# A relative position bias moved from VectorE into the score matmuls, loaded by shifted reads, with some modulation chunks reordered

## The reference, cut to what matters

```python
bias = na_bias(na_rpb[l], in_win, dr_idx, dc_idx)     # [heads, 256 queries, 256 keys], from a 15 x 31 table per head
ya = merge_heads(na_latent(qa, ka, va, ka_c, va_c, bias, row_idx))
```

## Time and profile before

| what | before |
|---|---|
| median of 3 runs | 1964.91 us (1964.04 to 1965.57) |
| the profiled execution: time, span | 1964.91 us, 1963.0 us |
| TensorE busy | 1861.0 us (95%) |
| GpSimd busy | 1359.7 us (69%) |
| ScalarE busy | 935.7 us (48%) |
| VectorE busy | 737.9 us (38%) |
| share of TensorE in the chain that ended last | 85% |
| mean granted TensorE clock | 0.985 |

### The profile page before, as it was taken

One profiled execution on the slowest core, in us unless ns is written; L12 is line 12 of the kernel. 1 busy time (PEld: TensorE's weight loads), 2 busy tenths in 40 slices (PEclk: granted clock), 3 DMA queues, 4 the chain that ended last, 5 costly groups with the idle time before them and its releaser, 6 DMA issues.

```text
span 1963.0 us, 28180 instructions
## 1 busy us (share of the span) xinstructions
PE 1861.0 (95%) x9518; PEld 1483.9 (76%) x9518; DVE 737.9 (38%) x1323; ACT 935.7 (48%) x1464; POOL 1359.7 (69%) x780
## 2 busy tenths in 40 slices
PE   7987999989899999999999999999999899999997
PEld 5665788776688888677888886778888776778886
DVE  2276443257421125345111446452113646451112
ACT  4454544353454455565444545644445445644442
POOL 5504999650488878656988795478886884469883
PEclk9999999999999999999999999999999999999999
DMA  7747666567776655434766453346664453246661
GB/s 251 247 172 254 196 194 202 171 198 252 241 229 192 192 171 161 145 117 135 220 201 190 155 178 97 97 140 192 205 190 151 151 161 106 88 140 191 184 189 67
DMA packets 245560, 344.24 MB, mean 175 GB/s; under 512 B 20704, under 2 KB 140384, under 8 KB 245472
## 3 DMA queue, kind: packets, MB, share of 16 engines
q1 hardware_dynamic: 243328, 337.06, 54.1%
q10 hardware_dynamic: 2144, 6.03, 1.0%
HBM read 341.96 MB, written 1.05 MB: 175 GB/s over the span
## 4 chain that ended last, share of the span: by engine, by line
PE 85%; DVE 7%; ACT 3%; DMA 1%; issue 1%; POOL 1%; SPq 0%; ACTq 0%; DVEq 0%
PE bank L1990 24%; PE bank L1992 23%; PE bank L1991 23%; PE bank L2061 2%; PE bank L2536 2%; PE bank L2526 2%; PE bank L2553 2%; PE bank L2040 1%; ACT wh L671 1%; DVE xh L1185 1%; PE bank L2072 1%; PE bank L2229 1%; DVE xl L1187 1%; PE bank L2309 1%; DMA raw<-in_l_w_in 1%
## 5 line engine op out<-in xcount | busy, mean ns | idle before, releaser
L647 POOL TENSOR_TENSOR wl<-raw,wh 128x1024 fp32r<-128x1024 f32 x300 | 732.1, 2454 | 87.7 <-ACT wh L809 76.9
L1990 PE MATMUL bank<-wh,xh 128*128 128x512 f32 (+2 forms) x1746 | 692.7, 397 | 21.6 <-POOL wl L633 8.7
L1992 PE MATMUL bank<-wl,xh 128*128 128x512 f32 (+2 forms) x1746 | 674.1, 386 | 0.0
L1991 PE MATMUL bank<-wh,xl 128*128 128x512 f32 (+2 forms) x1746 | 673.8, 386 | 0.0
L632 POOL TENSOR_TENSOR wl<-raw,wh 128x512 fp32r<-128x512 f32 (+2 forms) x238 | 325.3, 1367 | 489.3 <-ACT wh L671 450.3
L809 ACT ACTIVATE wh<-raw 128x1024 fp32r<-128x1024 f32 x270 | 286.4, 1061 | 439.0 <-PE bank L1992 429.3
L1990 PEld LDWEIGHTS bank<-wh,xh 128*128 128x128 f32 x1746 | 329.7, 189 | 98.8 <-issue 27.7
L1992 PEld LDWEIGHTS bank<-wl,xh 128*128 128x128 f32 x1746 | 329.6, 189 | 68.0
L1991 PEld LDWEIGHTS bank<-wh,xl 128*128 128x128 f32 x1746 | 330.2, 189 | 62.0 <-issue 1.4
L671 ACT ACTIVATE wh<-raw 128x1024 fp32r<-128x1024 f32 (+2 forms) x268 | 274.2, 1047 | 206.9 <-PE bank L1992 134.5
L633 POOL TENSOR_TENSOR wl<-raw,wh 128x512 fp32r<-128x512 f32 (+2 forms) x238 | 318.2, 1337 | 0.0
(11 more groups left out here) (316 smaller groups left out, 1677.1 us busy)
## 6 DMA issues: line engine op xcount, KB each, us to landing
raw<-in_w_ffn_in SPq DMA_DIRECT2D x264, 256.0 KB, 2.9
raw<-in_w_in SPq DMA_DIRECT2D x224, 256.0 KB, 2.9
raw<-in_w_mod SPq DMA_DIRECT2D x192, 256.0 KB, 3.9
raw<-in_w_ffn_out SPq DMA_DIRECT2D x132, 256.0 KB, 2.9
raw<-in_l_w_gate SPq DMA_DIRECT2D x88, 256.0 KB, 3.7
raw<-in_l_w_up SPq DMA_DIRECT2D x88, 256.0 KB, 4.3
raw<-in_l_w_down SPq DMA_DIRECT2D x88, 256.0 KB, 2.9
raw<-in_l_w_in SPq DMA_DIRECT2D x48, 256.0 KB, 4.4
```

What stands on the lines that cost most here:

```text
L647: nc.gpsimd.tensor_tensor(wl[:, s, :], raw[:, s, :], words(wh)[:, s, :], ALU.subtract)\
L1990: mm(dst, x_hi, w_hi, start=first, stop=False, skip_group_check=True)
L1991: mm(dst, x_lo, w_hi, start=False, stop=False, skip_group_check=True)
L1992: return mm(dst, x_hi, w_lo, start=False, stop=last, skip_group_check=True)
```

## The change

1. The host passes the raw table (`rpb`, 2 x 8 x 15 x 31 floats) instead of the expanded one. `load_bias` reads it with overlapping rows: for each head two DMAs, each to 64 partitions, of 6 x 64 floats per partition. Partition p begins one float later than partition p-1, so queries come out in reversed order within each half of 64. That makes 16 DMAs for a layer in runs of 256 bytes, instead of 4 in runs of 3072 bytes.
2. A constant `flip` (two 64 x 64 exchange matrices) turns the order back. In every near step of the x streams two matmuls (128 x 128 by 128 x 256, float32) with `flip` write the bias into the two banks, and the score matmuls on the x keys add to that (`start` false). The additions and their waits on VectorE go. TensorE waits for `bias_set` ahead of the first score.
3. Modulation chunks of layer 1: 4 instead of 6 ahead of `mix1`, 2 in every `mla` step (two more in all), none within `out1` (four fewer), 8 instead of 4 in `mod1_norm`. One chunk of `uq` is computed ahead of the turn of the second latent, and ScalarE's limits for its copies follow.

```diff
+    put("flip", np.kron(np.eye(2), np.eye(64)[::-1]))
+    w, u = 63 - np.arange(P)[:, None] % 64, np.arange(64)[None, :]
...
-    plan.modulation("mod1_in", 1, w_mod[1], 6)
+    plan.modulation("mod1_in", 1, w_mod[1], 4)
...
-        plan.modulation(f"mod1_mla{u}", 1, w_mod[1], 1 if u in (2, 8) else 2)
-    plan.gemm("out1", a["l1_w_out"], [512] * 2, pair=0, k_groups=[range(2, KD), range(0, 2)], modulated={0: each[0]})
-    plan.modulation("mod1_norm", 1, w_mod[1], 4)
+        plan.modulation(f"mod1_mla{u}", 1, w_mod[1], 2)
+    plan.gemm("out1", a["l1_w_out"], [512] * 2, pair=0, k_groups=[range(2, KD), range(0, 2)])
+    plan.modulation("mod1_norm", 1, w_mod[1], 8)
...
-                act.dma_start(bias[:, heads, :, :].rearrange("p h d u -> p h (d u)"), a["rpb"][l, :, heads, :]).then_inc(bias_in, 16)
+                for h in heads:
+                    for half, dr in ((0, 5), (1, 4)):
+                        at = (l * NAH + h) * RPB_R * RPB_C + dr * RPB_C + RPB_C // 2 - 63
+                        src = bass.AP(a["rpb"].tensor, at, [[1, 64], [RPB_C, 6], [1, 64]])
+                        act.dma_start(bias[64 * half:64 * half + 64, h, :, :], src).then_inc(bias_in, 16)
...
-                    if s == XS and u < 2 * NAH:
...
-                        step(v.tensor_tensor(own, own, near, ALU.add))
-                        settle()
...
+            latent_chunk("uq", 1)
             latent_turn(1)
             drive(1)
-            latent_chunk("uq", 1)
...
-                mod_chunk(plan.tiles["out1"][0][2][part][0] + 1)
...
+                            pe.wait_ge(bias_set, l + 1)
...
+                    local = near and s == XS
+                    if local:
+                        for e in range(2):
+                            mm(unit_bank(2 * i + e)[:, 0:SEQ], C_("flip"),
+                               bias[:, 2 * h + e, 2 - 2 * qb:6 - 2 * qb, :].rearrange("p a b -> p (a b)"), start=True, stop=False,
+                               skip_group_check=True)
```

More of the change, by code:

```diff
@@ L44 @@
        ("q_gain_1", 64), ("k_gain_1", 64)]
-CON = [("ident", 128), ("colmask", 64), ("cos_a", 16), ("sin_a", 16),
+CON = [("ident", 128), ("flip", 128), ("colmask", 64), ("cos_a", 16), ("sin_a", 16),
        ("cos_d", 64), ("sin_d", 64), ("cos_x", 64), ("sin_x", 64), ("modsum", 48), ("count", 16)]
@@ L71, in constants @@
     put("ident", np.eye(P))
-    w, u = np.arange(P)[:, None] % 64, np.arange(64)[None, :]
+    put("flip", np.kron(np.eye(2), np.eye(64)[::-1]))
+    w, u = 63 - np.arange(P)[:, None] % 64, np.arange(64)[None, :]
     start = np.clip(w - 8, 0, 48)
@@ L128, in blocks @@
         return out.reshape(P, SSM_J * P)
-    q, j, u = (np.arange(n) for n in (P, 6, 64))
-    row, col = (5 - q // 64)[:, None, None] + j[None, :, None], RPB_C // 2 + u[None, None, :] - (q % 64)[:, None, None]
-    near = np.asarray(x["na_rpb_2"])[:, :, row, np.clip(col, 0, RPB_C - 1)].transpose(0, 2, 1, 3, 4)
     return {
@@ L141, in lay_out @@
         "x": np.asarray(x["x"]).reshape(SEQ, D), "ctx": np.asarray(x["ctx_2"]).reshape(SEQ, D),
-        "rpb": np.ascontiguousarray(near).reshape(2, P, NAH, 6 * 64),
+        "rpb": np.asarray(x["na_rpb_2"]).reshape(-1),
         "post": np.stack([np.asarray(x[n]) for n in ("l0_mix_post", "l0_ffn_post", "l1_mix_post", "l1_ffn_post",
@@ L967, in _ @@
             tail("in1")
-            hi_until(plan.tiles["uq"][2][2][0][0] + 1)
+            hi_until(plan.tiles["uq"][1][2][0][0] + 1)
             evac_latent(1)
@@ L1036, in _ @@
             nc.scalar.activation(zv, yv, ACT.Gelu_apprx_tanh).then_inc(z_gelu, 1)
-            hi_until(plan.tiles["out1"][1][2][2][0] + 1)
+            hi_until(plan.first["out1"] + RING)
             act.wait_ge(z_glu, 1)
@@ L1150, in half_block @@
                     act.wait_ge(xt_split, split_at[f"m_{name}"] + 4)
-                ffn(f"ffn_{name}", sg2, [lambda h=h: load_bias(("c0", "x0").index(name), slice(h, h + 2)) for h in range(0, NAH, 2)]
+                ffn(f"ffn_{name}", sg2, [lambda h=h: load_bias(("c0", "x0").index(name), (h, h + 1)) for h in range(0, NAH, 2)]
                     if name != "x1" else [], ahead)
@@ L1852, in half_block @@
                     if s == XS and what == 4:
-                        dve.wait_ge(bias_in, 16 * NAH // 2 * (l + 1))
+                        dve.wait_ge(bias_in, 16 * 2 * NAH * (l + 1))
                         table = bias.rearrange("p h d u -> p (h d) u")
@@ L2439, in _ @@
             x_ready("out1", 1)
-            tile_chunk("out1", 0, 3)
-            mod_chunk(plan.tiles["out1"][0][2][3][0] + 1)
-            tile_chunk("out1", 1, 3)
+            for i in range(2):
+                tile_chunk("out1", i, 3)
             modulate("mod1_norm")
@@ L2525, in scores @@
                             rhs = kT[k][r, h, :] if near else gkT[k][r, h // 2, :]
-                            ins = mm(unit_bank(2 * i + e)[:, SEQ * n:SEQ * n + SEQ], lhs, rhs, start=n == 0, stop=True,
+                            ins = mm(unit_bank(2 * i + e)[:, SEQ * n:SEQ * n + SEQ], lhs, rhs, start=n == 0 and not local, stop=True,
                                      skip_group_check=True)
```

## The result

The changed kernel took 1982.18 us in the median (1980.58 to 1985.52, 8 runs), the kernel before 1965.24 beside it (8 runs). The ratio is 1.0078, with a 95% interval of 1.0057 to 1.0099: slower by 11 to 19 us. The forecast was 1970.0, with a range up to 1976.5. The sign was right, the size was not, and the time lies outside the range.

What follows compares the result with a forecast made beforehand. TensorE, busy for 95% of the span, was taken as the bound. Flips +6.7, modulation chunks -1.6 and bias loads 0 gave +5.1 on 1964.9, so 1970.0 us, with an 8-in-10 range of 1964.5 to 1976.5.

Steps and rivals of the forecast that it cites:

- The flips: Near steps of x0 and x1: two flip matmuls of 0.43 us a step, partly covered by waits, +3.36 a layer, 6.7 in all.
- Rival 1: Near steps: all 32 flips exposed because the waits move with the scores, 13.8 less 1.6, 1977.1 us; chance 0.10.
- the waits of 0.44, 1.40 and twice 1.24: TensorE's waits in a layer's near steps, claimed to shrink and cover part of the flips' time.
- Steps 0 to 3: First four near steps of a layer: flips claimed to cost 1.64 us, set by VectorE reaching the 1.40 wait later.
- a price of 0.66: Upper bound for one flip, 0.43 plus a change of 0.23: 5.8 a layer, both 11.6; sets the range's end, 1976.5.
- `out1` and `mla`: Modulation chunks: four fewer in `out1` save 2.97 us; two more in `mla` cost 0.48, one of them hidden in a wait.
- The bias loads: Feed forward steps: 24 more DMA issues at 0.35 us or somewhat more, packets at 0.070, all hidden; cost 0.
- Rival 2: Short bias runs starve the weights in eight feed forward steps, 1 us showing each time, 1978 us; chance 0.10.
- The stream ... I take 0.5: Entry of `ffn1`: late modulation and weight chunks delay ScalarE's copy and the norm by up to 1.3 us, taken as 0.5.
- ScalarE, not the turn, sets the pace: Norm at `ffn1`: ScalarE's copies, up to 1.3 us late, set the time, so a faster row turn gains nothing there.
- the 0.4 for ScalarE: End of `out1`: ScalarE's squares and roots of tile 0 may take back up to 0.80 us of the saving, taken as 0.4.
- The third rival: Entry of `ffn1`: eight chunks keep the clock up, 2.4 us gained, -4.9 with modulation, flips almost hidden, 1961 us; chance 0.08.

Runs made afterwards that it cites:

- experiment 4: Kernel before with only the bias loads changed to 32 DMAs in short runs, additions still on VectorE, no flips: ratio 0.9995 (0.9982 to 1.0008).
- experiments 5 and 9: Kernel before with second `uq` chunk ahead of the turn: with ScalarE's lowered limit (5) ratio 1.0038; with limit left as it was (9, second kernel) 1.0019.
- experiment 6: Changed kernel with six modulation chunks ahead of `mix1` and six in `mod1_norm`, in place of four and eight: 1981.27 us, ratio 1.0093.

## Why the prediction was right or wrong

- **The flips: the mechanism right, the size 0.5 a layer low.** 0.86 a step was taken, and the lag grows by 0.87 over step 1, or by 1.06 in steps 0 and 5. (From the flips' start to the scores' it is 0.96 in step 1 and 1.82 with four flips, so two flips are 0.86.) Rival 1, with all cover gone, is out: the waits of 0.44, 1.40 and twice 1.24 covered about what the prediction said they would, and steps 6 and 7 cost nothing. Steps 0 to 3 cost 1.9 in place of 1.64, steps 4 and 5 1.9 in place of 1.72. The term was 3.36 a layer, measured 3.8. One of the prediction's bounds was added up wrongly: at a price of 0.66, TensorE by itself comes 2.64 + 0.88 + 1.32 - 1.40 = 3.44 later in steps 0 to 3, and by the prediction's own rule this counts and not 3.02. Both layers are then 12.5, not 11.6, and the range would end at 1977.4, still below the measured time.
- **`out1` and `mla`: right**, -2.97 against -3.05 and 0.48 against 0.45.
- **The bias loads: right in the sum**, 0 against 0. The price of an issue, "0.35 or somewhat more", was 0.65. The packets were cheaper than taken: queue 10's 13792 took 1.8% of 16 engines' span, 0.041 us each, where 0.070 was taken. Rival 2 is out by experiment 4.
- **"`uq`" has no term: the first failure.** The prediction took up the bias, the chunks and the loads, but not the moved chunk of `uq` with ScalarE's limit, though the description of the change names both. Leaving it out put it at nothing without a reason. Behind the lowered limit stands the copy that the third chunk needs. ScalarE's row of the kernel before has it start at 433.89, as soon as its weights had landed and ahead of the latent at 434.65; it would have shown that the lowered limit puts that copy behind the latent. The cost was 6.9 us, more than the whole forecast: in the kernel before about 4.9 by the limit and 1.65 by the order (experiments 5 and 9).
- **"The stream ... I take 0.5": the second failure.** The prediction saw the ring of six, and that chunks seven and eight are issued late. It let chunk eight land 5.6 after the end of `out1`; it was there at 544.17, 10.5 after. It was issued about when the prediction had it, but took 8.5 us to land and not 3.9, which is a median over the whole kernel. Here the DMA engines had first stood idle, behind a ring full of unused chunks, and then had eight DMAs of `ffn1`'s weights queued behind the chunk's own, 1.06 busy. That these eight slow it is read from the order in time; no run takes them apart. "ScalarE, not the turn, sets the pace" held in experiment 6, but at 4.15, not 1.3. With the 0.4 for ScalarE the term was 0.9, measured 5.6. Of the 12.5 us between the forecast's sum (5.1) and the measured one (17.6), `uq` makes 6.9, this term 4.7 and the flips 0.9.
- **The clock.** The third rival had eight chunks keep it up; in the trace it fell to 0.50 in the wait of 5.58 between chunks seven and eight. So the rule of the page "TensorE: Matmul & The Clock Gate" of the Trainium skill (Part 1), that idleness halves the clock, agrees with the trace; the rival's premise of eight chunks without a gap did not hold. The same 0.50 is a part of why a wait of 4.11 in `uq` went with a cost of 6.9.

## What to carry to other kernels

Give every hunk of a diff a term of the sum, the one-line limits of another engine's queue first: ask what stands behind the instruction that the engine now reaches earlier, and who needs it. Work that fills a wait is free only if its data don't push the next stage's data out of the ring. Count slots, not microseconds: at this boundary four chunks were free, and the next two cost 3.1 to 3.65. And one profile is one draw here: compare stage by stage, and look for operations of ten times their usual length, before a difference of 3 us is laid to a change.

## What was unexpected of the hardware

- VectorE's addition of 0.69 us took 10.39 in four of the profiles, and an operation that took 2.56 in another execution took 16.52 in one of them, until GpSimd's gapless run ended. More often both engines got slower together (1.67 for the 0.69, and 1.74 for GpSimd's 1.28). It cost 2.9 to 11.6 us of the total each time, and it moved from one execution of the same kernel to the next.
- A DMA of 384 runs of 256 bytes took 0.65 us to issue in the median and up to 2.28, against 0.33 for one of 384 KB in long runs; 32 of them cost the kernel nothing.
- The wait in brackets understates what a wait covers: scores to turn shrank from 2.37 to 1.07 and the turn from 1.32 to 1.09 where all waiting was gone, 1.53 in all for a wait named as 1.24.
